# Eighteen weight chunks of the first projection beside the conditioning units, with partial sums in SBUF

## The reference, cut to what matters

```python
mod = silu(c) @ ada_w + ada_b                    # 2048 x 12288 weights, 9 conditioning vectors
sh1, sc1, g1, sh2, sc2, g2 = split(mod, 6)
h = rms_norm(x) * (1.0 + sc1) + sh1              # x / sqrt(mean(x*x)) over 2048 features
proj = h @ w_in                                  # 2048 x 18448: hq, hf, hi, hg, mq, mk, mv, mi, mf, mo, ga, gb
... HGRN2 heads from hq, hf, hi, hg, ga; mLSTM heads from mq, mk, mv, mi, mf, mo, gb
x = x + g1 * ((merged heads) @ w_out)
... second norm, conv FFN, x + g2 * ff, final norm
```

## Time and profile before

| what | value |
|---|---|
| median of 3 runs | 2286.97 us (2285.03 to 2287.28) |
| profiled execution, its span | 2286.7 us |
| PE busy | 2227.3 us, 97% |
| VectorE busy | 1091.9 us, 48% |
| ScalarE busy | 992.9 us, 43% |
| DMA | 460.03 MB, mean 201 GB/s |

### The profile page before, as it was taken

The page is one execution under the profiler, slowest core; times in us unless marked ns, Lnnn a source line. Parts: engine busy times, 40 slices in busy tenths (PEclk is TensorE's granted clock), DMA queues, the critical chain, the costliest instruction groups (busy, mean ns, idle before and its releaser), DMA issues. The chain is left out here.

```text
span 2286.7 us, 42270 instructions
## 1 busy us (share of the span) xinstructions
PE 2227.3 (97%) x17436; PEld 2084.4 (91%) x17436; DVE 1091.9 (48%) x1454; ACT 992.9 (43%) x1365; POOL 319.4 (14%) x455
## 2 busy tenths in 40 slices
PE   6899999999999999999999997999999999999998
PEld 2489999999999999999999986999999999999997
DVE  1245455464464544444444555555555555544443
ACT  3245553563554334444434445443444343433333
POOL 1010212211221222120211223000000000110000
PEclk8899999999999999999999999999999999999999
DMA  9977676666656576766675779555555555555553
GB/s 344 366 242 220 182 211 186 205 187 206 211 183 198 178 231 194 237 213 205 202 233 180 227 240 317 179 159 172 160 168 160 168 162 166 176 164 172 169 169 107
DMA packets 407411, 460.03 MB, mean 201 GB/s; under 512 B 14844, under 2 KB 379956, under 8 KB 406434
## 3 DMA queue, kind: packets, MB, share of 16 engines
q1 hardware_dynamic: 394192, 410.64, 57.9%
q0 software_dynamic: 12240, 46.03, 6.5%
q10 hardware_dynamic: 833, 1.26, 0.2%
HBM read 431.48 MB, written 26.39 MB: 200 GB/s over the span
## 5 line engine op out<-in xcount | busy, mean ns | idle before, releaser
L697 PE MATMUL ps<-xh,whi 128*128 128x288 f32 x3968 | 1193.4, 301 | 9.8 <-issue 6.2
L1575 DVE TENSOR_TENSOR wlo<-raw,whi 128x1024 fp32r<-128x1024 f32 x584 | 731.3, 1254 | 977.2 <-ACT whi L1161 968.2
L699 PE MATMUL ps<-xh,wlo 128*128 128x288 f32 x3968 | 1172.2, 295 | 0.0
L698 PE MATMUL ps<-xl,whi 128*128 128x288 f32 x3968 | 1171.2, 295 | 0.0
L1161 ACT ACTIVATE whi<-raw 128x1024 fp32r<-128x1024 f32 x584 | 616.5, 1057 | 803.2 <-PE ps L699 773.1
L697 PEld LDWEIGHTS ps<-xh,whi 128*128 128x128 f32 x3968 | 746.7, 188 | 63.2 <-issue 58.9
L698 PEld LDWEIGHTS ps<-xl,whi 128*128 128x128 f32 x3968 | 746.8, 188 | 0.0
L699 PEld LDWEIGHTS ps<-xh,wlo 128*128 128x128 f32 x3968 | 746.5, 188 | 0.0
L697 PE MATMUL ps<-ffh,whi 128*128 128x288 f32 x704 | 209.2, 297 | 0.0
L699 PE MATMUL ps<-ffh,wlo 128*128 128x288 f32 x704 | 208.4, 296 | 0.0
L698 PE MATMUL ps<-ffl,whi 128*128 128x288 f32 x704 | 208.3, 296 | 0.0
(11 more groups left out here) (393 smaller groups left out, 1583.6 us busy)
## 6 DMA issues: line engine op xcount, KB each, us to landing
raw<-in_w_in SPq DMA_DIRECT2D x288, 512.0 KB, 4.3
raw<-in_w_up SPq DMA_DIRECT2D x176, 512.0 KB, 3.6
raw<-in_w_down SPq DMA_DIRECT2D x88, 512.0 KB, 3.5
araw<-in_ada_w SPq DMA_DIRECT2D x74, 512.0 KB, 5.4
raw<-in_w_out SPq DMA_DIRECT2D x32, 512.0 KB, 3.5
uraw_x<-in_ada_w SPq DMA_DIRECT2D x30, 512.0 KB, 8.7
uraw<-in_ada_w SPq DMA_DIRECT2D x24, 512.0 KB, 10.2
top<-in_ada_w SPq DMA_DIRECT2D x24, 512.0 KB, 8.0
```

The source lines that it names most:

```text
L697: mm(o, whi[:, s, kk, cols], hi[:, kt0 + kk, :], start=first and kk == 0, stop=False)
L698: mm(o, whi[:, s, kk, cols], lo[:, kt0 + kk, :], start=False, stop=False)
L699: x = mm(o, wlo[:, s, kk, cols], hi[:, kt0 + kk, :], start=False, stop=last and kk == KC - 1)
L1575: TT(wlo[:, s], raw[:, s], whi[:, s].bitcast(F32), ALU.subtract).then_inc(lo_done, 1)
```

## The change

Eighteen chunks instead of six run beside the units, from unit 2 on instead of unit 3. The order of chunks changes: the first 24 chunks are blocks 0 to 5, quarter by quarter (six chunks for quarter 0, six for quarter 1, and so on). Each of these 24 chunks is a sum of its own in PSUM; ScalarE copies the first six into `SQ`, and VectorE adds the other 18 to it (`early_add`). Behind them blocks 6 to 9 run as before. The list behind chunk 18 has three chunks for each pair of `a` instead of five. The hooks move: gates from 10 to 19, `gate_rows` from 14 to 23, `hg_front` by five, and the eviction of block 6 from chunk 27 to chunk 30. The squares come from rows of `x` (ScalarE, with a sum over the row), and PE spreads them with a diagonal matrix; VectorE now copies the transposed tiles. POOL's write of `xT` moves from behind unit 7's third group to behind unit 1.

```diff
-EARLY = 6
-HG_FIRST = "s" * EARLY + "sssssaa" * 6 + "ssss"
+EARLY = 18
+PARTED = 24
+HG_FIRST = "s" * EARLY + "sssaa" * 6 + "ssss"
...
-    return (n % 2, n // 2) if first and n < 8 else (n // length, n % length)
+    return (n % 6, n // 6) if first and n < PARTED else (n // length, n % length)
...
-BESIDE = 3
+BESIDE = 2
...
-EARLY_PIECES = (0, 1, 1, 2, 1, 1, 1, 1, 0, 1, 1, 2, 1, 1, 1, 1, 0, 2, 2, 2)
+EARLY_PIECES = (1, 2, 2, 2, 3, 3, 3, 3, 3, 2, 3, 3, 3, 3, 3, 3, 3, 3, 3, 3, 3, 2, 2, 2)
+EARLY_LOADS = 20
...
+    return RING if u == BESIDE else min(EARLY_LOADS, 2 * RING + pieces_ahead(u - 1, c // 2) // 4)
...
-GATES = 10
+GATES = 19
+ROWS = 23
+FRONT = 5
...
+                        if start and q < PARTED:
+                            pe.wait_ge(bank_free[q % 2], q // 2 + FREE)
+                            chunk(q + 1, q, True, True, q % 2, xh, xl, KC * s, steps, 4 if q == EARLY else None)
...
+            for t in range(3):
+                w = P if t < 2 else TS
+                if t == 2:
+                    act.wait_ge(sq_done, 1)
+                A(junk[0:w, D * (t % 2):D * (t % 2 + 1)], xtm[0:w, t, :], ACT.Square, accum_out=ssx[0:w, t:t + 1]).then_inc(sq_done, 1)
...
-                    if part == 3 and evict is not None:
+                    if start and n < PARTED:
+                        pass
+                    elif start and n == PARTED + 6:
+                        act.wait_ge(used, N[0] + n - 2 + FREE)
+                        evict(6, 0)
+                    elif part == 3 and evict is not None and not (start and b == 6):
...
+            def early_add(n):
+
+                dst, src = early_tile(n), early_bank(n)
+                dve.wait_ge(used, n + 1 + FREE)
+                TT(dst[:, :, 0:TP], dst[:, :, 0:TP], src[:, :, 0:TP], ALU.add)
+                v = dst[:, :, TP:TPAD].rearrange("p m (j e) -> p m j e", e=32)[:, :, :, 0:2 * LS]
+                TT(v, v, src[:, :, TP:T].rearrange("p m (j e) -> p m j e", e=2 * LS), ALU.add).then_inc(bank_free[n % 2], 1)
...
+            def each(n):
+                if n < PARTED:
+                    early_add(n)
+            stream(N_HG, HG_FIRST, A_HG, hook, each, start=True)
...
             pool.wait_ge(x_c, KT + X_FREE)
-            pool.wait_ge(u_used, 4 * UNITS - 1)
+            pool.wait_ge(u_used, 4 * BESIDE)
```

More of the change, by code:

```diff
@@ L120 @@
 N_HG = (0, 0)
+FIRST_PAIRS = PARTED // 2 + 2
 def hg_base(i):
-    return ahead(N_HG, i, 40, 5)
+    return ahead((40, FIRST_PAIRS), i - 1, 40, 5) if i else N_HG
 N_ML = hg_base(4)
@@ L560, in stage @@
                     if kind == "s":
-                        if first and n < EARLY:
+                        if first and n < EARLY_LOADS:
                             continue
@@ L778, in stream @@
                         b, s = place(q, length, start)
[L779 to L785, removed]
+                        if start and q < PARTED:
+                            pe.wait_ge(bank_free[q % 2], q // 2 + FREE)
+                            chunk(q + 1, q, True, True, q % 2, xh, xl, KC * s, steps, 4 if q == EARLY else None)
+                        else:
+                            if s == 0:
+                                pe.wait_ge(bank_free[b % 2], N[1] + b // 2 + (PARTED // 2 - PARTED // 8) * start + FREE)
+                            if xparts is not None and b == 0:
+                                pe.wait_ge(xlo, xparts + s + 1)
+                            chunk(N[0] + q + 1, q, s == 0, s == length - 1, b % 2, xh, xl, kt0 + KC * s, steps, halves if q == 0 else None)
                     else:
@@ L1043, in _ @@
             pe.wait_ge(ada_free, UNITS + FREE)
[L1044 removed]
+            stream(hg_base(0), HG_FIRST, A_HG, late(GATES, gates(0, "", 0, 0)), start=True)
             pe.wait_ge(row_d, ROW_T)
@@ L1237, in conv_state @@
                 A(cst[:, :, 8 * g:8 * g + 8].rearrange("p f r -> p r f"), ab[:, 0:8 * FT].rearrange("p (r f) -> p r f", f=FT), ACT.Copy).then_inc(small_c, 1)
+            act.wait_ge(ld_x, 48)
+            for t in range(3):
+                w = P if t < 2 else TS
+                if t == 2:
+                    act.wait_ge(sq_done, 1)
+                A(junk[0:w, D * (t % 2):D * (t % 2 + 1)], xtm[0:w, t, :], ACT.Square, accum_out=ssx[0:w, t:t + 1]).then_inc(sq_done, 1)
             unit(0)
-            unit(1)
             act.wait_ge(const, 7)
@@ L1310, in stream, with hg_evict @@
                         each(n)
[L1312 to L1317, removed]
+            def hg_evict(g):
                 def evict(u, b):
[L1319 to L1322, removed]
+                    if u == 0:
                         act.wait_ge(hg["cp"], 2 * g)
-                    if u == 4 and not first:
+                    if u == 4:
                         act.wait_ge(hg["vc"], g)
```

209 lines of the change are left out of this document (121 added, 88 removed).

## The result

| | median, us | lowest to highest | runs |
|---|---|---|---|
| before | 2287.02 | 2285.03 to 2287.28 | 4 |
| after | 2307.14 | 2305.15 to 2308.49 | 4 |

The ratio is 1.0086, 95% interval 1.0071 to 1.01: the change makes the kernel slower by 20 us, outside the predicted range (2277 to 2298). The profiled execution of after has a span of 2302.9 us, 16.2 more than that of before. The first stage, which ends at ScalarE's last copy into `SG`, ends at 264.11 us instead of 247.51: 16.6 us later. So all that the two traces differ by is lost there.

A forecast was written before the change was run, and what follows sets the result against it. PE bounds the kernel behind 124 us, transfers bound the front; 2286.7 us minus 8.6 gained in the front plus 11.4 of new waits behind chunk 18 gives 2289.5 us, range 2277 to 2298.

The forecast's parts named there:

- Bound, front: Up to chunk 18: transfers bound the front, PE the rest; twelve more chunks run early, gaining 8.6 us (5 to 14).
- the write: In the front, before unit 3: writing `xT`, 2.36 MB, now falls among the transfers and costs 6.1 us.
- Squares and copies, adds in the units: Beside front transfers and units: squares and copies cost zero, 0 to 1 us either way; the 18 adds cost nothing.
- Chunk 23, VectorE's add: At chunk 23: PE waits 3.5 us for its bank, since VectorE converts chunk 24 before it adds chunk 21.
- Chunk 29, `wlo`: At chunk 29: PE waits 2.0 us for the low part, behind ScalarE's sigmoid, gates, silu, logarithms and exponentials.
- the turn: At the turn behind chunk 25: PE waits 0.5 us more for `arows`.
- Chunk 32, the copy into `SG`: At chunk 32: PE waits 5.4 us for block 6's bank, evicted behind chunk 33's conversion and the front's last step.
- the sum of what stands behind chunk 18: Behind chunk 18: new PE waits total 11.4 us, at least about 4 and at most 16.
- (B): Rival, behind chunk 18: ties are loose, only chunk 23 waits, 3 us; front gives 11; 2279 us; chance 0.27.
- (C): Rival, chunk 32: late block 6 eviction loses more than the front wins; waits 15 us, 2297 us; chance 0.33.
- T + 54: At block 6's eviction: T is when PE has used the first `a`, behind chunk 20; leaving later than this means slower.
- Its mark: At the first stage's end: ending over 4.6 us later would show the slower rival, chance 0.33.

The follow-up runs named there:

- e8: Changed kernel with the 2.36 MB write back behind unit 7's third group, writing eight tiles of `xh` instead of `xT`: 2304.59 us, ratio 1.0071 to before.
- e4: Kernel before with only the change's squares and copies: 2288.65 us, ratio 1.0002 to before.
- e9: Changed kernel with the gate rows eight chunks later and GpSimd's two gate stores behind its part of the front: 2308.25 us, ratio 1.0087 to before.
- e5: Changed kernel with `a` pairs three chunks later in SP's list, VectorE's `mod` earlier, and adds of chunks 20 to 23 before conversions: 2288.91 us, ratio 1.0002.
- e6: e5 plus the gate rows eight chunks later and GpSimd's two gate stores behind its part of the front: 2281.91 us, ratio 0.9971 to before.
- e3: Changed kernel with VectorE's `mod` ahead of the conversion and gate rows in the first stage: 2300.99 us, ratio 1.0054 to before.
- e7: Kernel before with one PE stall put in ahead of chunk 31, waiting for four GpSimd memsets: 2295.48 us, ratio 1.0024 to before.
- e10: Changed kernel with `a` pairs three chunks later in SP's list and the gate rows eight chunks later: 2285.35 us, ratio 0.9993 to before.
- e1: Changed kernel with VectorE adding before it converts at chunks 20 to 23: 2304.38 us, ratio 1.0064 to before.

## Why the prediction was wrong, step by step

- **Bound, front.** Right. Unit 3's first group 68.38 us (68.3), chunk 18 at 154.89 (153.7), the front gives 7.4 (8.6). Inside it the write was priced 1.6 us too high (e8), and something else in the front is that much dearer; what, the runs don't tell.
- **Squares and copies, adds in the units: nothing.** Right for the squares and copies (e4). The adds weren't tried alone; PE is busy 55.62 of the 56 us behind unit 3's start.
- **Chunk 23, VectorE's add: 3.5 us.** Right in place and kind, 4.24, since the load took 8.1 and not 7.3 us.
- **Chunk 29, `wlo`: 2.0 us and 0.5 at the turn.** Near in size, by luck. PE waits for no low part at chunk 29, and there is no gap at the turn. The gates' steps in ScalarE's list, from which I had worked out the 2.0, make PE wait nowhere there. The 1.37 us are at chunk 30, whose load is the late third one.
- **Chunk 32, the copy into `SG`: 5.4 us.** 5.28, and of the kind given, a load behind a pair, but one pair earlier than I had it. ScalarE waits 11.22 us for chunk 30; behind that stand the exponentials, chunk 32's conversion, the front's last steps and the copy. Chunk 33, which I had named, reached ScalarE at 226.72, and VectorE, still busy with the front, came to it 1.2 us after ScalarE was through. In e9, where chunk 30 comes earlier, it is chunk 33, as I had it. The copy left about 61 us behind the first `a` instead of 51, with PE late by as much. The gates were not in this term, rightly: e9 took them away and the wait stayed at 4.9; only with the loads in time are they what is late next (e5, e6).
- **The step that failed: the sum of what stands behind chunk 18, 11.4 us.** The priced waits came to 10.9, so the terms were nearly right. Two weren't there. The first is PE's second block of `a`, which waits for `mod`: 5.92 us. I went through VectorE's list for adds and low parts and not for `mod`, which stands in it behind a conversion, the gate rows and two scans; e3 shows its price. The second is the low clock behind gaps, 7.2 us. I had charged it in the front (2.7 us) and put it at nothing behind, without a reason; e7 shows it by itself. Together 24.0 instead of 11.4, against 7.4.
- **Rivals.** (B) is out: the ties hold. (C) had the sign right and decides "from a sum of waits of 13.4 us on", which the waits alone, 16.8, pass; but its 2297 us came from silu, gates and logarithms in line and from a poorer front, and neither is what happened. Block 6 did leave later than T + 54, but since PE was late too, the wait there was 5.28 us, less than the front won. Its mark, a stage that ends over 4.6 us later, came true with 16.6.

What stays open: how much of the loss belongs to the third reload's extra 4 us, which follow GpSimd's two stores of the gates; no run took the stores alone away. And where e9 lost the 4 us that its earlier copy had won.

## What to carry to other kernels

Where a ring shares its queue with loads that wait for a later use, count how many chunks cover the reload: here three (9.6 us) didn't cover 8 us and what is tied behind it, while five (16 us) did, and the order of one list was worth 19 of 20 us. Go through each in-order list for every instruction that frees something for the bound engine, not only for those that the change adds, and ask of each gap in a full PE stream what low clock follows it (here 3.5 us cost 6.2, while 3.2 cost just their length). Take ties away together before judging one: with the loads in time, singly two of them were worth nothing and 3.5 us, together 6.8, and the rows that were moved away from one `mod` stood ahead of the next.

## What the runs showed of the hardware

A gap of 3.52 us (e7) in a stream that had run at 2.4 GHz was followed by stretches at a mean clock of 0.53 and 0.61, then 1.00 again; in the changed kernel it was 0.53 and 0.62 behind the gap of 5.92 us, 0.50 and 0.70 behind that of 5.28 us, 0.60 behind that of 4.24 us. Each of these cost 1.6 to 3 us on top. But behind e5's gap of 3.34 us it was 0.68 and 0.90, which makes some 1.5 us, and behind e10's of 3.22 us every stretch stood at 1.00: that gap cost its length and no more.

Moving 2.36 MB out of a front that is full of transfers (387 GB/s) brought it forward by 4.5 us, less than the 6.1 that bytes over rate give. I hadn't expected that.

GpSimd's two stores of the gates' last values move 72 values of 4 bytes. In four kernels a stretch of a few us with a busy DMA and little moved begins 3 to 5 us after them, wherever they stand: 54 GB/s at a share of 1.05 in before (174 to 178 us, stores at 170.5 and 171.0), 104 at 0.97 in the changed kernel, 45 at 0.83 in e6 (228 to 232, stores at 223.5 and 224.1), 36 at 1.04 in e9 (252 to 256, stores at 249.4 and 250.0), where the long stretches above moved 348 and 387 GB/s at a share near 1. The reload that falls there takes 11.9 to 13.2 us (e8, changed kernel, e1) instead of 8.3 (e9). That the stores are the cause is argued from these places; no run shows it by itself.
